# Down projection of the second block's gated MLP: activations stationary, tokens on the partitions, and a last group finished one token half at a time

## What is computed

```python
def conv_ffn(h, w_up, conv_w, w_down):
    u = h @ w_up
    up = jnp.pad(u, ((0, 0), (CONV_WIDTH_2 - 1, 0), (0, 0)))
    c = conv_w[0] * up[:, 0:S]
    for j in range(1, CONV_WIDTH_2):
        c = c + conv_w[j] * up[:, j:j + S]
    gate, val = jnp.split(c, 2, axis=-1)
    return (jax.nn.silu(gate) * val) @ w_down        # w_down is 5632 x 2048

    x = x + rms_norm_2(conv_ffn(h, ...), norm_g[i, 3])
```

## Time and profile before

| | |
|---|---|
| median of 3 runs | 2322.53 us |
| the profiled execution | 2323.18 us |
| its span in the profile | 2321.4 us |
| TensorE busy | 2238.7 us (96%) |
| VectorE, ScalarE, POOL busy | 1609.9 (69%), 1097.9 (47%), 752.4 us (32%) |
| TensorE's granted clock, mean | 0.986 of full |
| DMA | 407.34 MB, 175 GB/s on average |

### The profile page before, as it was taken

How to read it: one execution, slowest core, us unless ns; L and a number is a source line. 1 busy time by engine, 2 the same in 40 slices (tenths; PEclk the granted TensorE clock), 3 DMA queues, 4 the chain that set the end, 5 groups by cost and what they waited for, 6 DMA issues and landing times.

```text
span 2321.4 us, 38150 instructions
## 1 busy us (share of the span) xinstructions
PE 2238.7 (96%) x12956; PEld 1953.8 (84%) x12956; DVE 1609.9 (69%) x2001; ACT 1097.9 (47%) x1627; POOL 752.4 (32%) x751
## 2 busy tenths in 40 slices
PE   8999889999999999999999999979999999999995
PEld 7888758888888888888899877867888888888885
DVE  7676575656666666666687666787785678767876
ACT  5344354544454354354466455454553455434552
POOL 4121003452142142133445122235540154413433
PEclk9999899999999999999999999989999999999998
DMA  6557204555555555555555643534555555555552
GB/s 238 181 176 238 93 1 151 190 179 199 187 187 188 189 190 189 190 182 190 181 191 182 207 167 126 172 119 150 203 190 191 189 188 184 190 190 190 190 189 92
DMA packets 115141, 407.34 MB, mean 175 GB/s; under 512 B 12464, under 2 KB 16848, under 8 KB 115056
## 3 DMA queue, kind: packets, MB, share of 16 engines
q1 hardware_dynamic: 110592, 401.64, 51.2%
q10 hardware_dynamic: 4464, 4.61, 0.7%
HBM read 404.05 MB, written 2.15 MB: 175 GB/s over the span
## 4 chain that ended last, share of the span: by engine, by line
PE 87%; DVE 6%; POOL 3%; issue 2%; ACT 2%; DMA 0%; POOLq 0%; SPq 0%; DVEq 0%; ACTq 0%
PE bank L406 49%; PE bank L413 26%; PE bank L420 1%; PE bank L422 1%; PE bank L421 1%; PE bank L506 1%; DVE wboth L771 1%; POOL bias L1580 1%; PE bank L465 1%; PE bank L467 1%; PE bank L466 1%; ACT Sm L1313 1%; PE bank L678 1%; DVE Sm L1198 1%; ACT wboth L1268 0%
## 5 line engine op out<-in xcount | busy, mean ns | idle before, releaser
L771 DVE TENSOR_TENSOR wboth<-raw,wboth 128x1024 fp32r<-128x1024 f32 x757 | 1033.7, 1367 | 446.8 <-ACT wboth L1268 446.1
L1268 ACT CAST wboth<-raw 128x1024 fp32r<-128x1024 f32 x757 | 788.2, 1048 | 773.4 <-PE bank L406 383.0
L406 PE MATMUL bank<-A,wboth 128*128 128x512 f32 x3200 | 775.5, 394 | 14.8 <-DVE A L846 9.1
L406 PEld LDWEIGHTS bank<-A,wboth 128*128 128x128 f32 x3200 | 590.4, 190 | 134.1 <-issue 16.6
L406 PE MATMUL bank<-H,wboth 128*128 128x512 f32 x2304 | 558.4, 392 | 0.3 <-DVE z L802 0.3
L406 PEld LDWEIGHTS bank<-H,wboth 128*128 128x128 f32 x2304 | 421.6, 189 | 84.0 <-issue 3.4
L413 PEld LDWEIGHTS bank<-A,wboth 128*128 128x128 f32 x3200 | 413.9, 192 | 29.9 <-DVE wboth L771 6.9
L413 PE MATMUL bank<-A,wboth 128*128 128x256 f32 x3200 | 421.9, 284 | 9.9 <-DVE wboth L771 5.5
L413 PEld LDWEIGHTS bank<-H,wboth 128*128 128x128 f32 x2304 | 298.9, 191 | 14.2 <-issue 1.0
L413 PE MATMUL bank<-H,wboth 128*128 128x256 f32 x2304 | 305.4, 283 | 0.0
L802 DVE TENSOR_REDUCE z<-bank 128x256 f32<-128x512 f32 x284 | 195.7, 689 | 88.8 <-PE bank L406 86.9
(11 more groups left out here) (219 smaller groups left out, 1611.6 us busy)
## 6 DMA issues: line engine op xcount, KB each, us to landing
raw<-wstream SPq DMA_DIRECT2D x757, 512.0 KB, 3.2
bias<-bias_rows ACTq DMA_DIRECT2D x6, 512.0 KB, 5.1
x<-xT SPq DMA_DIRECT2D x4, 512.0 KB, 6.8
out<-x SPq DMA_DIRECT2D x3, 512.0 KB, 2.7
pA<-bias_rows ACTq DMA_DIRECT2D x2, 512.0 KB, 8.6
out<-x SPq DMA_DIRECT2D x2, 256.0 KB, 2.0
Sm<-pT ACTq DMA_DIRECT2D x1, 256.0 KB, 2.6
con<-consts SPq DMA_DIRECT2D x1, 254.0 KB, 10.2
```

Of the source, the lines that this page charges most:

```text
L406: last = nc.tensor.matmul(bank(j)[:, :], whi[:, s, cols(i)], moving(j, k), start=(k == 0), stop=(k == K - 1))
L771: V.tensor_tensor(wlo[:, s, :], raw[:, s, :], whi[:, s, :].bitcast(F32), ALU.subtract).then_inc(lo_ready, 1)
L1268: C.copy(whi[:, s, :], raw[:, s, :]).then_inc(hi_ready, 1)
```

## The change

All three down stages take the second form. `H` is stationary, 128 tokens at a time; four weight tiles of one row move. A group f is 512 output features for both token halves, so `dn0` and `dn1` are 4 groups of 8 pieces, `dn2` 4 groups of 6. `y` and the residual are now tokens by features (`yN`, `xN`), and so is the output. Evacuations are one operation of 128x512 per group and token half, copied in `dn0` and added in `dn1` and `dn2`, all on VectorE; POOL adds nothing any more. The host lays out the weights of these stages to suit, and passes g3 as a row, which ScalarE loads to all partitions by a transfer at the start of `dn2`.

In `dn2` TensorE also turns the residual `x` in 8 sets of 4 transposes, one after each of four pieces in groups 0 and 1; ScalarE copies each bank to `xN`. ScalarE squares each evacuated part with a sum along the row, POOL multiplies parts 0 to 2 by the gain. The sum over the features is now a sum of 4 numbers per token, so the matmul with ones goes, and root, inverse and refinement work on 128x1. In the last group both token halves go together for 2 pieces (FIN_SPLIT = 4 tiles of `H`); then half 0 takes the remaining 4 pieces, and after it half 1 the same 4. VectorE finishes half 0 after `dn_half`, half 1 after the last piece. Each half goes out in 4 transfers.

```diff
-    STAGES += [(f"up{_c}", 2 * _n, 16), (f"dn{_c}", 16, _n)]
+    STAGES += [(f"up{_c}", 2 * _n, 16), (f"dn{_c}", 8, _n)]
@@ SyncE
-            for a, b in FIN_CHUNKS:
...
-                sp.dma_start(out[:, a:b, :], x[:, a:b, :]).then_inc(out_done, 16)
+            for t in range(QT):
+                for f in range(4):
+                    sp.wait_ge(fin_out, 4 * t + f + 1)
+                    w = slice(f * WIDE, f * WIDE + WIDE)
+                    sp.dma_start(out[:, t, w], xN[t][:, w]).then_inc(out_done, 16)
@@ TensorE
+                def down2(it, f):
+                    p = it * n + f * n // 2 + PB[dn]
...
+                    for t in range(QT):
+                        pe.wait_ge(z_ready, u + t + 1)
+                    def rows_of(k, t):
...
+                        nc.tensor.matmul(bank[:, :], H[:, k, 0, tok], whi[:, s, w], start=(k == 0), stop=False)
+                        nc.tensor.matmul(bank[:, :], H[:, k, 0, tok], wlo[:, s, w], start=False, stop=False)
+                        return nc.tensor.matmul(bank[:, :], H[:, k, 1, tok], whi[:, s, w], start=False, stop=(k == n - 1))
+                    final = n < CH and it * 2 + f == 3
+                    for k in range(FIN_SPLIT if final else n):
+                        pe.wait_ge(up_ready, t0 + k + 1)
+                        if k % 2 == 0:
+                            pe.wait_ge(lo_ready, p + (k // 2 + 1))
+                        for t in range(QT):
+                            last = rows_of(k, t)
+                        if k % 2 == 1:
+                            last.then_inc(piece_used, 1)
+                            if n < CH:
+                                turn_x(it * 2 + f, k // 2)
+                    if final:
+                        for k in range(FIN_SPLIT, n):
+                            if k % 2 == 0:
+                                pe.wait_ge(lo_ready, p + (k // 2 + 1))
+                            last = rows_of(k, 0)
+                        last.then_inc(dn_half, 1)
+                        for k in range(FIN_SPLIT, n):
+                            last = rows_of(k, 1)
+                            if k % 2 == 1:
+                                last.then_inc(piece_used, 1)
+                def turn_x(f, q):
+                    i = 4 * f + q - 2
+                    if f > 1 or q < 2 or i >= 2 * QT * 2:
+                        return
+                    if i >= 4:
+                        pe.wait_ge(x_copied, i - 3)
+                    t, c = i % QT, i // QT
+                    for d in range(4):
+                        last = nc.tensor.transpose(psum[4 + i % 4][:, d * P:d * P + P], x[:, 4 * c + d, t * P:t * P + P], ident)
+                    last.then_inc(x_turned, 1)
-            norm("end")
@@ VectorE
+                def down2_in(it, f):
+                    for t in range(QT):
+                        dst = yN[:, t, ds((it * 2 + f) * WIDE, WIDE)]
+                        bank = psum[(UB[dn] + 2 * f + t) % 4][:, :]
+                        if c == 0:
+                            V.tensor_copy(dst, bank).then_inc(z_ready, 1)
+                        else:
+                            V.tensor_tensor(dst, dst, bank, ALU.add).then_inc(z_ready, 1)
+                def down2(it, short=0):
+                    for q in range(LEAD, n + AHEAD):
+                        if AHEAD <= q < n + AHEAD - short:
+                            split_lo(it * n + PB[dn] + q, (PB[dn] + q) % SLOTS)
+                        for f in range(2):
+                            if n < CH and it == 1 and f == 1:
+                                continue
+                            if q - LEAD == (f + 1) * n // 2 - 1:
+                                dve.wait_ge(piece_used, it * n + (PB[dn] + SLOTS + q - LEAD + 1))
+                                down2_in(it, f)
-            norm(rs[:, :], 8).then_inc(rs_ready, 1)
...
+            st = Steps(dve, fin_step)
+            dve.wait_ge(in_g3, 16)
+            dve.wait_ge(x_copied, 8)
+            for t in range(QT):
...
+                if t == 0:
+                    dve.wait_ge(dn_half, 1)
+                else:
+                    dve.wait_ge(piece_used, SLOTS + NPIECE)
+                V.tensor_tensor(yN[:, t, w], yN[:, t, w], psum[(UB["dn2"] + 2 + t) % 4][:, :], ALU.add).then_inc(z_ready, 1)
+                dve.wait_ge(z_ready, 4 + UB["end"] - 1 + t)
+                V.tensor_tensor(lastg[:, t, :], yN[:, t, w], g3row[:, w], ALU.mult).then_inc(dn_scaled, 1)
+                dve.wait_ge(dn_sq, 7 + t)
+                st(V.tensor_reduce(fvar[:, c], ssq[:, t, :], AX, ALU.add))
+                V.tensor_scalar(fvar[:, c], fvar[:, c], 1.0 / D, EPS, ALU.mult, ALU.add).then_inc(var_ready, 1)
...
+                rsqrt(frs[:, c], fvar[:, c], 8 + t).then_inc(fin_rs, 1)
...
+                dve.wait_ge(dn_pooled, 6)
+                for f in range(4):
+                    w = slice(f * WIDE, f * WIDE + WIDE)
+                    V.scalar_tensor_tensor(xN[t][:, w], lastg[:, t, :] if f == 3 else yN[:, t, w], frs[:, c], xN[t][:, w],
+                                           ALU.mult, ALU.add).then_inc(fin_out, 1)
@@ ScalarE, dn2
+                    def copy_x(i):
+                        act.wait_ge(x_turned, i + 1)
+                        C.copy(xN[i % QT][:, i // QT * WIDE:i // QT * WIDE + WIDE], psum[4 + i % 4][:, :]).then_inc(x_copied, 1)
+                    def square3(t, f):
+                        act.wait_ge(z_ready, 4 + UB[dn] + 2 * f + t + 1)
+                        C.activation(..., yN[:, t, f * WIDE:f * WIDE + WIDE], ACT.Square,
+                                     accum_out=ssq[:, t, f:f + 1]).then_inc(dn_sq, 1)
+                    act.dma_start(g3row, grow.partition_broadcast(P)).then_inc(in_g3, 16)
+                    for q in range(2 * n):
+                        if 2 <= q and q + LEAD < 2 * n:
+                            split(PB[dn], PB[dn], q + LEAD, 0, 0)
+                        f, h = divmod(q, n // 2)
+                        if f < 2 and h > 2:
+                            copy_x(4 * f + h - 3)
+                        if f in (1, 2) and h == 0:
+                            copy_x(4 * f - 1)
+                        if f and f < 4 and h == 0:
+                            for t in range(QT):
+                                square3(t, f - 1)
+                    warm(ACT.Sqrt)
+                    for t in range(QT):
+                        square3(t, 3)
+                        root(8 + t, frs[:, t:t + 1], fvar[:, t:t + 1])
@@ POOL, after dn2
+            for f in range(3):
+                w = slice(f * WIDE, f * WIDE + WIDE)
+                for t in range(QT):
+                    pool.wait_ge(dn_sq, 2 * f + t + 1)
+                    G.tensor_tensor(yN[:, t, w], yN[:, t, w], g3row[:, w], ALU.mult).then_inc(dn_pooled, 1)
```

More of the change, by code:

```diff
@@ L70 @@
 for _c, _n in enumerate(CHUNKS2):
-    STAGES += [(f"up{_c}", 2 * _n, 16), (f"dn{_c}", 16, _n)]
+    STAGES += [(f"up{_c}", 2 * _n, 16), (f"dn{_c}", 8, _n)]
 PB, UB, ZB = {}, {}, {}
-NZ = {"gate": 0, "cv": 0, "vb": 0, "v2": 0, "misc": 1, "proj": 0, "wo2": 0, "dn0": 0, "dn2": 0}
+NZ = {"gate": 0, "cv": 0, "vb": 0, "v2": 0, "misc": 1, "proj": 0, "wo2": 0, "dn0": 0, "dn1": 0, "dn2": 0}
 _p = _u = _z = 0
@@ L756, in _ @@
+                if n == CH:
+                    with pe.Fori(0, 2) as it:
+                        for f in range(2):
+                            down2(it, f)
                 else:
                     for it in range(2):
[L758 to L759 removed]
+                        for f in range(2):
+                            down2(it, f)
@@ L1235, in _ @@
                     hidden2()
-                if n == CH:
[L1237 to L1241, removed]
+                def down2_in(it, f):
[10 more added lines that the diff above has]
+                            split_lo(it * n + PB[dn] + q, (PB[dn] + q) % SLOTS)
+                        for f in range(2):
+                            if n < CH and it == 1 and f == 1:
[3 more added lines that the diff above has]
+                                down2_in(it, f)
+                if n == CH:
+                    with dve.Fori(0, 2) as it:
                         down2(it)
@@ L1549, in _ @@
                 if n == CH:
-                    body(PB[dn], PB[dn], 0, 4, n, mixed=1)
-                    with act.Fori(1, 4) as it:
-                        body(it * 8 + PB[dn], PB[dn], it, 4, n)
-                else:
[L1554 to L1559, removed]
+                    with act.Fori(0, 2) as it:
+                        body(it * n + PB[dn], PB[dn], it, 8, n)
+                else:
+                    def copy_x(i):
[3 more added lines that the diff above has]
+                        act.wait_ge(z_ready, 4 + UB[dn] + 2 * f + t + 1)
+                        C.activation(zr[:, 2 * t:2 * t + 2, :].rearrange("p a b -> p (a b)"), yN[:, t, f * WIDE:f * WIDE + WIDE], ACT.Square,
+                                     accum_out=ssq[:, t, f:f + 1]).then_inc(dn_sq, 1)
```

(9 more changed lines are left out.)

58 lines of the change are left out of this document (31 added, 27 removed).

## The result

The changed kernel has a median of 2303.72 us (2301.96 to 2304.46, 4 runs) against 2321.38 us for the kernel before, timed beside it (2319.95 to 2323.21, 4 runs): 17.7 us less, a ratio of 0.9922, 95% interval 0.9907 to 0.9937. A second measurement gave 2303.77 (5 runs) against 2321.52 (15 runs), ratio 0.9927, interval 0.9913 to 0.9940. The sign and the main parts were forecast; the time of 2306.1 was 2.4 us too high, and 2303.72 lies just under the low end of 2303.8.

A forecast was written before the change was run, and what follows sets the result against it. TensorE's matmul pace in 88 pieces and 24.0 us behind them were taken as the bound. Pace -5.5, transposes +3.9 and an end of 9.2 instead of 24.0 gave -16.4 us: 2306.1 from 2322.53, range 2303.8 to 2312.0.

The forecast's parts named there:

- The pace of the new form: Down stages dn0, dn1, dn2: 12 matmuls of 512 columns a piece, 2.722 us, save 5.5 us together.
- Transposes: 32 new transposes on TensorE in dn2, 8 sets of 4, cost 0.49 us a set, 3.9 us in all.
- What was costed at nothing: Splitting, evacuations, squares, copies, POOL's products, g3's load and the last group's four held pieces stay hidden; a late piece costs about 1 us.
- The end: Behind TensorE's last matmul: VectorE's chain for two token halves, then transfers, takes 9.2 us instead of 24.0.
- The low bound of 8.6: Low value in us for the end behind TensorE's last matmul, with 0.692 a product.
- The high bound: High value for the end, 10.7 us: transfers queue by 0.7 and small steps cost 0.1 more each.
- the 13.5 us of scaling: VectorE's 16 tiles of scaling at the kernel's end: they go, and half of that now lies under TensorE.
- The base: Starting time for the forecast: the median of 2322.53 us, the profiled execution being 0.65 above it.
- (1): Rival: the new form brings nothing in the down stages, pieces still take 2.78 us; 2311.6 us, chance 0.08.
- (2): Rival: half 0's chain at the end is not hidden under TensorE, 5.5 us more; 2311.6 us, chance 0.07.
- (3): Rival: no gain in pace, half 0 not hidden, and a few exposed evacuations; 2319 us, chance 0.03.
- (4): Rival: transposes let TensorE's clock fall in dn2, 24 us over 10 pieces; 2330.1 us, slower by 7.6, chance 0.04.

## Why the prediction was right and wrong

**The pace of the new form: right.** 5.5 us were forecast; with the transposes taken out dn2 saves 66.88 - 65.28 = 1.6, dn0 and dn1 2.06 each, 5.7 in all. The reason given, a cost of 13 to 15 ns per matmul beyond its columns, was tested by putting four matmuls a piece back: the gain went with them, at 16.6 ns each. That the whole of it is a fixed cost of each matmul is not shown, as said there.

**Transposes: right.** 3.9 forecast, 3.87 measured. That it is so close is partly luck: a set was put at 0.40 + 0.09 and is 0.35 + 0.08, with 0.05 more in the spacings after it that was not in the sum. The transposes are dearer than what dn2 gains from the new form, so that stage alone grew by 2.3 us.

**What was costed at nothing: right.** No wait of TensorE shows from dn0 to the end; dn2 has the same length, 69.15 us, with and without the four pieces held for the early half.

**The end: right in mechanism, 0.7 us off in size.** 9.2 were forecast, 8.5 came. The step that failed is "Four products of 512 with a scalar from memory, 0.746 each": the duration was exact (0.743 to 0.752), but in a row of such operations the next begins before the record of the last ends, so the price is the spacing of 0.67. Four of them take 2.66 us in half 0 and 2.74 in half 1 instead of 2.98. The steps before them take 2.95 instead of 3.1. Since half 0's chain outlasts TensorE, its excess counted as well: 0.3 us instead of 0.65, and half 1 5.7 instead of 6.1. For TensorE the prediction had gone by starts, for VectorE it went by durations. The trace of before held the distance, on the very instruction from which the 0.746 was taken:

```profile
228.13 1.41 DVE L831 TENSOR_SCALAR vN<-bank,rcol 128x512 f32<-128x512 f32 x2
```

Two operations of 0.746 end to end would be 1.49 us; they fill 1.41, so the second began 0.66 after the first. The low bound of 8.6 does not follow from its own terms: 0.692 a product, in both halves, gives 8.8. The high bound counted the dearer small steps once; in both halves they make it about 11.3. And the 13.5 us of scaling were put down to what "now lies under TensorE"; the larger part went by one operation in the place of two, 8.1 us.

**The base: the step that failed for the most.** "From 2322.53 the forecast is 2306.1": this took the median of three runs as the kernel's time. 11 and 15 later runs put it at 2321.5, 1.0 lower, inside a spread of 3.7 us (2319.72 to 2323.44) that the three values shown, 3.0 apart, had already hinted at. The profile read for it was one of the two in which the clock fell at 26 us. The forecast difference of -16.4 on a base of 2321.4 would have been 2305.0; the measured median was 1.3 below that, of which 0.7 is the end, 0.2 the pace, and the rest is within the scatter. The range was built from the unknown costs of the change alone: taken as differences to 2322.53 it goes from -18.7 to -10.5 us, and the measured -17.7 lies inside it. On a base of 2321.4 its low end would have stood at 2302.7.

**The rivals.** (1) and (2) at 2311.6 did not come: the new form held the pace of rows 4 over 32 pieces, and the early half was hidden. What (2) describes was made by hand in the run without the early half and cost 5.4 us, against the 5.5 given. (3) needed both and did not come either. (4) did not come: the granted clock was 1.00 over the whole of dn2, transposes included.

## What to carry to other kernels

At equal columns count matmuls: here each one fewer was worth 16 to 17 ns, so moving 512 columns of weights past standing activations beats mixing 512 and 256, as long as the transposes that the new layout asks for cost less than the stage saves. A normalization at the end of a kernel was much cheaper here with the tokens on the partitions: root and inverse are one column wide (2.0 us), and, worth more (8.1 us), one operation scales by the root and adds the residual. Half of it can hide behind the other half's matmuls if the slots hold the pieces of both.

For a forecast, price a row of operations by the distance of their starts, on every engine, and put the scatter of the base's own runs into the range.

## What the hardware showed unexpectedly

VectorE's products of 512 last 0.745 us each but follow each other at 0.67. With one POOL addition of 512 beside it such a product lasted 1.77 us instead of 0.745 (0.94 instead of 0.48 for 256 before the change), and the addition is itself 1.7 long, where POOL's six products of the same size in dn2 had a mean of 1.37. Splitting one of three matmuls into two of 256 columns slowed its neighbours more than itself: from the pair to the next matmul it is 230 ns on average over 128 of them, 3.7 more than one of 512, while the step into the pair and the one after it are 233, 6 more each. And one and the same code reached dn0 anywhere within 2.3 us, latest where the clock, already up, fell to 0.50 from 26 to 29 us.
